# Two modulation blocks leave the log-gate stage of the linear attention for the place behind the output product's norm, and the square root's table is loaded before the squares

## The reference, cut to what matters

```python
# first block
mod = silu(c) @ w_ada[layer] + b_ada[layer]            # 6 x 1024 numbers: shift, scale, gate twice
g_f = log_sigmoid((lf @ w_decay[0] + b_decay[0])) / GATE_NORM      # the linear attention's log gates
g_b = log_sigmoid((lb @ w_decay[1] + b_decay[1])) / GATE_NORM
b_cum = jnp.cumsum(to_chunks(g), axis=3)
qe = qc * jnp.exp(b_cum)                               # kc * exp(-b_cum), kc * exp(b_last - b_cum)
...
out_lat = merge_branches(...)                          # ... @ w_out
x_lat = x_lat + gt1 * mix
h = modulate(rms_norm(x_lat, norm2_g[layer]), sh2, sc2)
x_lat = x_lat + gt2 * conv_ffn(h, w_up, conv_w, conv_b, w_down, rows, GRID_W)
# second block, for each of its two layers
m = silu(cond) @ w_mod[i] + b_mod[i]                   # for c_2 and c_ctx_2
h = modulate_2(x, g_norm1[i], m[..., 0, :], m[..., 1, :])
```

## Time and profile before

| | us |
|---|---|
| three runs: median (lowest, highest) | 1830.57 (1829.31, 1833.48) |
| profiled execution: its own time, given as its span from first to last instruction | 1825.3 |
| PE busy | 1549.9 (85% of the span) |
| DVE busy | 668.0 (37%) |
| ACT busy | 394.2 (22%) |
| the chain that ended last: PE, DMA, DVE, ACT | 59%, 33%, 4%, 2% |

### The profile page before, as it was taken

How to read it: one execution, slowest core, us unless ns; L and a number is a source line. 1 busy time by engine, 2 the same in 40 slices (tenths; PEclk the granted TensorE clock), 3 DMA queues, 4 the chain that set the end, 5 groups by cost and what they waited for, 6 DMA issues and landing times.

```text
span 1825.3 us, 21752 instructions
## 1 busy us (share of the span) xinstructions
PE 1549.9 (85%) x8872; PEld 983.8 (54%) x8872; DVE 668.0 (37%) x1501; ACT 394.2 (22%) x710; POOL 46.5 (3%) x64
## 2 busy tenths in 40 slices
PE   6989999989999999997987777767797968676766
PEld 4544568878888877766443433334453524242433
DVE  3267566648898356676210101000222100010102
ACT  4222341011220024232221211111222211121211
POOL 0000000000110000001000000000000000000000
PEclk9999999999999999998897889888997988888888
DMA  9535854874549924215799999999987999999996
GB/s 366 198 129 184 309 204 156 305 262 176 201 168 341 351 94 172 96 59 240 320 429 427 429 429 428 429 428 428 413 348 308 430 428 429 428 428 429 428 428 290
DMA packets 110828, 572.52 MB, mean 314 GB/s; under 512 B 9188, under 2 KB 15460, under 8 KB 86184
## 3 DMA queue, kind: packets, MB, share of 16 engines
q1 hardware_dynamic: 109776, 569.79, 77.4%
q10 hardware_dynamic: 984, 1.79, 0.3%
HBM read 570.51 MB, written 1.05 MB: 313 GB/s over the span
## 4 chain that ended last, share of the span: by engine, by line
PE 59%; DMA 33%; DVE 4%; ACT 2%; SPq 1%; issue 1%; DVEq 0%; ACTq 0%
DMA ring<-in_w_exp_up_dram 32%; PE bank L494 18%; PE bank L1291 10%; PE bank L976 9%; PE bank L1005 4%; PE bank L502 2%; PE bank L1317 2%; PE bank L1371 2%; PE bank L1023 2%; PE bank L1327 1%; PE bank L1278 1%; PE bank L650 1%; DMA ring<-in_w_ada_dram 1%; PE bank L708 1%; PE bank L660 1%
## 5 line engine op out<-in xcount | busy, mean ns | idle before, releaser
L1291 PE MATMUL bank<-ring,arena 128*32 128x512 f32 x1792 | 259.4, 732 | 185.7 <-DMA ring<-in_w_exp_up_dram 183.8
L1291 PEld LDWEIGHTS bank<-ring,arena 128*32 128x32 f32 x1792 | 66.9, 131 | 374.7 <-issue 222.9
L2712 DVE COPY arena<-bank 128x256 f32<-128x256 f32 x32 | 13.6, 425 | 571.6 <-PE bank L1307 571.6
L976 PE MATMUL bank<-hT,ring 128*128 128x256 f32 x704 | 156.1, 384 | 4.2 <-ACT hT L1561 4.2
L976 PEld LDWEIGHTS bank<-hT,ring 128*128 128x128 f32 x704 | 135.3, 193 | 25.1 <-issue 6.2
L1317 PE MATMUL bank<-ring,arena 128*32 128x512 f32 x960 | 129.9, 688 | 1.9 <-DVE arena L2716 1.9
L1905 ACT COPY arena<-bank 128x512 f32<-128x512 f32 x32 | 33.4, 1045 | 432.2 <-PE bank L1291 432.2
L494 PE MATMUL bank<-ring,hT 128*128 128x512 f32 (+2 forms) x320 | 124.3, 543 | 0.0
L1327 PE MATMUL bank<-arena 128*128 128x256 f32 x512 | 119.0, 385 | 1.8 <-DVE arena L2724 1.8
L1327 PEld LDWEIGHTS bank<-arena 128*128 128x128 f32 x512 | 94.6, 190 | 41.1 <-issue 29.6
L1278 PE MATMUL bank<-arena 128*128 128x32 f32 x960 | 109.9, 274 | 0.0
(11 more groups left out here) (372 smaller groups left out, 1609.0 us busy)
## 6 DMA issues: line engine op xcount, KB each, us to landing
ring<-in_w_exp_down_dram SPq DMA_DIRECT2D x60, 2048.0 KB, 18.5
ring<-in_w_exp_gate_dram SPq DMA_DIRECT2D x56, 2048.0 KB, 19.2
ring<-in_w_exp_up_dram SPq DMA_DIRECT2D x56, 2048.0 KB, 23.7
ring<-in_w_mod_dram SPq DMA_DIRECT2D x16, 2048.0 KB, 14.5
ring<-in_w_ada_dram SPq DMA_DIRECT2D x12, 2048.0 KB, 13.8
ring<-in_w_up_dram SPq DMA_DIRECT2D x10, 2048.0 KB, 11.5
ring<-in_w_in_dram SPq DMA_DIRECT2D x8, 2048.0 KB, 14.2
arena<-in_w_mod_dram SPq DMA_DIRECT2D x8, 2048.0 KB, 8.2
```

The costliest lines, as they stand in the source:

```text
L976: ins = pe.matmul(b[:, 0:T], x[:, k, j * 128:j * 128 + 128], hT[:, k, 0:T], start=(k == 0), stop=(k == KD - 1))
L1291: ins = pe.matmul(bank[0][32 * q:32 * q + 32, :], xe[:, k * CAP:(k + 1) * CAP], xs[q // 2][:, o:o + 512], start=(k == 0), stop=(k == KD - ...
```

## The change

- PE's list: blocks 14 and 15 are no longer computed behind gr; block 13 alone is turned there. Their two products stand behind the norm's last matmul and ahead of the up product, in banks of the second half. Their turns follow tiles 1 and 3 of the up product. `mod(i)` is split into `mod_product` and `mod_turn`, and `pending` is now taken from its front.
- ACT: the copies of blocks 14 and 15 move to tiles 0 and 2 of the up stage. The first Exp of bc now also waits for all eight of `log_gates`, as its output overwrites the last `z_low`. A one-element square root is added ahead of the squares, so that the table for it is loaded there.
- DVE: the sums of blocks 14 and 15 move to tiles 2 and 4.
- SP: the weights of 14 and 15 are loaded behind those of the output product and the beside blocks 22 and 23, ahead of the first up weights. Each of the items behind gr up to there moves two places forward in the ring.

```diff
-ROWS_ORDER = [0, 1, 2, 3, "g0", 12, 13, 14, 15, "g1", "g2", "g3", "g4", "g5", "g6"]
+ROWS_ORDER = [0, 1, 2, 3, "g0", 12, 13, "g1", "g2", 14, 15, "g3", "g4", "g5", "g6"]
...
     cols("gr", w_in, IN_GR, 512)
-    for _ in range(2):
-        mod(next(mods))
+    late = [next(mods) for _ in range(2)]
...
     for g in range(2):
         rows(("w_out", g), w["w_out"][0], 512 * g, 4)
+    for i in late:
+        mod(i)
...
             def mod_turn(second=False):
-                i = pending.pop()
+                i = pending.pop(0)
...
             def mod(i):
 
+                mod_product(i)
+                if len(pending) > 1:
+                    mod_turn()
+
+            def mod_product(i, second=False):
+
                 x = w3(weights(pe, ("mod", i)), KD, 512)
-                b = G.open(pe, ("mod", i))
+                b = G.open(pe, ("mod", i), second)
...
                 G.close(ins, ("mod", i))
                 G.over(("mod", i))
-                if pending:
-                    mod_turn()
                 pending.append(i)
...
             G.over("gr")
-            mod(14)
-            mod(15)
             mod_turn()
...
             outputs_and_norm(2, way_out)
             G.over(("w_out", 0), ("w_out", 1))
+            for i in (14, 15):
+                mod_product(i, second=True)
...
+                    if 4 * g + j in (1, 3):
+                        mod_turn(second=True)
...
-            send(before[first_out:first_up], first_out)
+            send(before[first_out:after_out], first_out)
             for n in range(6, 8):
                 send_beside(n)
-            send(before[first_up:], first_up)
+            send(before[after_out:], after_out)
...
                 act.activation(g, g, ACT.Ln, bias=one).then_inc(sem("gate_log"), 1)
-            mod(14)
-            mod(15)
...
                         act.wait_ge(done, G.number[("ke",) + ((tb, 0) if d else (tb - 1, 1))])
+                    else:
+                        act.wait_ge(sem("log_gates"), 8)
...
+            act.activation(small[:, 4:5], one, ACT.Sqrt)
             squares(2, xT, lambda k: G.read(act, ("wo", k)))
...
+                if j in (0, 2):
+                    mod(14 + j // 2)
...
             evict(("gr", 3), grT[:, 3, :], T)
-            for i in (13, 14, 15):
-                mod(i)
+            mod(13)
...
                 ins.then_inc(sem("conv_done"), 1)
+                if j in (2, 4):
+                    mod(13 + j // 2)
```

More of the change, by code:

```diff
@@ L1436, in send_beside @@
                     sem(f"beside_in_{n % 2}"), 16)
-            first_out, first_up = sequence.index(("w_out", 0)), sequence.index(("up_gate", 0))
+            first_out, after_out = sequence.index(("w_out", 0)), sequence.index(("mod", 14))
             send(before[5:first_out], 5)
```

## The result

The changed kernel takes 1819.12 us (median of 6 runs, 1816.83 to 1825.91) where the kernel before takes 1831.17 in the same rounds (6 runs, 1829.31 to 1833.48). The ratio is 0.9949, with a 95% interval from 0.9936 to 0.9962, so 7 to 11.7 us faster. The forecast was 1822.5, range 1818.5 to 1826.5. A second set with more runs gave 1823.72 (12 runs, 1819.05 to 1826.8) against 1829.52 (31 runs): ratio 0.9966, 0.9952 to 0.9979, or 3.8 to 8.8 us.

A forecast was written before the change was run, and what follows sets the result against it. TensorE (59% of the chain) and the work ahead of the experts' weight stream were taken as the bound. 5.55 + 0.59 + 0 + 2.87 - 0.88 = 8.13 us off 1830.57 gave 1822.5 us, range 1818.5 to 1826.5.

The forecast's parts named there:

- Log-gate stage: First Exp of bc, waiting last for all eight log gates, starts at 236.03 instead of 241.59: 5.55 us gained.
- The bank wait of aft: In the log-gate stage, aft waits for the bank of gr's last tile: costed at nothing, at most 0.4 us.
- Table load: At the output product's norm, the root no longer waits for its table load: 0.59 us gained, not 1.28.
- 2.1 us more by the Trainium skill: At the norm's table load, the skill page's load plus drain, 2.66 us a switch, would give 1820.4.
- Products: Two moved products, 3.70 us, fit into TensorE's wait behind the norm's last matmul: cost 0, upper bound 3.5.
- the margin of 0.16 us: Behind the norm, time to spare between the two products' end at 404.57 and hT's first tile at 404.73.
- Clock: First up tiles: with the idle time filled, TensorE's clock stays at its upper level: 2.87 us gained, bounds 0 to 2.87.
- Turns: Up stage: two turns among its tiles at 0.44 us each cost 0.88 us.
- Later loads: Up and down stages: weights issued later, such as block 24 and up gate weight 1, still arrive in time: nothing.
- The slower rival: Up stage: up gate weight 1 lands too late in front of tile 4, giving 1834.3 us; chance 0.03.
- Gain lost on the way: Up to the experts: their weight stream is bound by its own bytes, giving 1830.6 us; chance 0.05.
- Another low-clock stretch vanishes: Further on, as later waits fall at other times: some 3 us more, 1819.5 us; chance 0.08.

The follow-up runs named there:

- the second execution: The kernel after run once more with nothing edited, and profiled again: 1823.72 us (12 runs).
- the kernel after with two waits filled: Kernel after plus unread matmuls in the grouped attention and ahead of the pooling layer's input product: 1819.44 us, ratio to before 0.9945.

## Why the prediction was right

The place and the size of each step came out. That the first median fell 3.4 us below the forecast is luck of the executions as far as the traces go: in the one that was profiled two low-clock stretches are missing, which was among the rivals; the second set gained 5.8 us between the medians, less than forecast.

- **Log-gate stage, 5.55 forecast.** The first Exp of bc moved from 241.59 to 235.97; less the 0.10 us by which the execution was ahead at g0, 5.52. The condition named as the last one, all eight log gates, is the one in the chain. Where only the Exp's wait is moved, 0.40 us more comes out, which makes 5.9, just above that part's bounds (5.1 to 5.8): bc then decides, as reckoned. The bank wait of aft cost nothing.
- **Table load, 0.59 forecast.** 0.59 by taking it out, 0.58 by adding it alone. Half of the load lay behind the matmul of the sum. By the Trainium skill (page "ScalarE: Activation LUTs", section "What ACT_TABLE_LOAD costs") a drain of 1.38 us would have gone with it; the trace doesn't show this here: in the kernel without the early load it runs from 394.97 for 1.28 us and the root starts at 396.26. The prediction's estimate of 2.1 us more by the Trainium skill forgot that half of the load is hidden, as it reckons itself: 0.59 + 1.38 us would be 1.4 us more, so 1821.1.
- **Products, 0 forecast.** The up product starts 0.03 us behind them, so of the margin of 0.16 us little was left. They still don't set its start: ACT's first shift starts at 398.47 and with the 0.52 of the earlier trace rows ends at 398.99, and the up product follows 0.13 us later, as in the kernel before (405.19 and 405.32). With the products moved away it starts 228.42 us behind g0, with them 228.43.
- **Clock, 2.87 forecast.** 2.85 in the kernel before with unread products, which move no work; lost again, with 3.2, when the products leave the wait. Forecast and measurement start from the same profile of the kernel before, so that they agree to 0.02 says only that the upper level was reckoned rightly (41.59 and 41.61); what the low clock costs differs from one execution to the next, 1.7 to 3.2 us in the three with a wait of 3.6 to 4.2.
- **Turns, -0.88 forecast.** 42.49 in the kernel after against 41.61 with the clock up and no turns: -0.88.
- **Later loads, 0 forecast.** No wait on a weight up to 450 us.
- **The slower rival** (up gate weight 1 late) didn't occur: no wait at tile 4. **Gain lost on the way** was wrong in its main claim: g3 to the experts is 426.22 in the second execution against 426.25 before, so what is won ahead of 450 us arrives at 870. Behind that 1.1 to 1.5 us can be lost: in the five profiles where the experts' first 64 records take 9.7 to 9.8 us (9.79 after, against 8.38 before, both at a low clock at first) the last expert's product with its scatter matrix comes that much later than in the kernel before. In all twelve profiles the time from the end of those 64 records to it is 419.7 to 420.1 us, whether they take 8.4 or 9.8, so that what they lose is not made up later. It is the execution and not the moved blocks: the kernel before with the table alone has 9.77 and 429.51, the kernel after with two waits filled 8.45 and 428.39. What holds the rest of the stream at a fixed length was not tested; in those five TensorE waits 1.4 to 1.5 us for the last down weight (1293.08 above).
- **Another low-clock stretch vanishes**, given 0.08, is what the first profile shows: the one around 722 us (1.67 us from g3 to the experts) and the one in the pooling layer's input product (29.40 to 27.70). Against the second profile it has nothing of the sort. So this belongs to the execution and not to the change.

The sum for the profiled execution: 0.10 to g0, 8.07 to g3, 1.67 to the experts, -1.36 to the end of the last one, 2.02 behind it, together 10.50 us, and TensorE's last row moved from 1815.83 to 1805.33.

What stays open is which condition decides whether a wait of about 2 us drops the clock: a wait of 1.89 us ahead of the pooling layer's product is followed by 27.70, 29.40 or 30.50 us, one of 2.25 us in the grouped attention by a low clock in eight of ten profiles, and a wait of 2.33 us behind the norm was followed by a clock of 1.00 in its one profile.

## What to carry to other kernels

A wait of TensorE can cost twice: itself, and a stretch at half the clock behind it. Here independent work of 3.7 us put into a wait of 4.2 us cost nothing and gave back 2.85 us of clock, on top of the 5.5 us at the place that it left; placed behind the tiles instead (the first product 14 us later) the same work ate all but 1.14 us of the gain. Where there is no work to move, products that nobody reads do the same for the clock, in the waits of about 2 us here; in the longer waits of the router they did not.

When the runs of one kernel spread by more than the effect, cut the profiles into stages at fixed rows and subtract: 8.07 us was to be seen from one execution each, where 12 runs against 31 left it between 3.8 and 8.8. Still profile both kernels more than once: two profiles of the kernel after agree to 0.01 us, but a low-clock stretch inside the stage, as in the kernel before, makes its length a matter of the execution.

## What the runs showed of the hardware that was not expected

- Behind one and the same wait of 1.89 us (the pooling layer's input product, 64 records) TensorE ran at the upper level at once or at the lower one at first, from execution to execution: of ten profiles without a filling there two show 27.70 us, five 29.40 and three 30.47 to 30.50. The kernel after lies at both ends. With one product of 1.92 us put into the wait it was 27.70 and 27.71.
- The low clock, not the chip's transfers, is then most of what differs between two executions of one kernel where both have a trace: at least 4.4 of 7.5 us (1.64 and 2.80), and 6.1 with the 1.65 us in the latent attention.
- A matmul of a product's shape keeps its time right behind the norm's wait of 0.59 us: 3.64 us for 32 records, on weights (L527) as on constants (L971).
